# Where GpSimd's modulation units stand in a fused two-block transformer kernel

## The chip, the cores and the metric

The kernel runs on one core of one Trainium2 chip. The metric is the time of one execution in microseconds (us) on the device. Engines are called by their names: TensorE (PE, its weight loads PEld), VectorE (DVE), ScalarE (ACT), GpSimd (POOL), SyncE (SP, which here only issues transfers).

## The reference

Two transformer blocks follow each other on 256 tokens of width 1024, all in float32. Both are modulated: a vector `c` gives, through `silu(c) @ w_ada + b_ada`, the shift, the scale and the gate of every sublayer.

```python
# first block
sh1, sc1, gt1, sh2, sc2, gt2 = split(silu(c) @ w_ada + b_ada, 6)
p = project(modulate(rmsnorm(x, g_mix), sh1, sc1))       # q, k, v, g, decays, convolution, gates
x = x + gt1 * merge_branches(gla_bidir(p), conv(p))      # gated linear attention, both directions
x = x + gt2 * swiglu(modulate(rmsnorm(x, g_ffn), sh2, sc2))
x = rmsnorm(x, g_final)
# second block: nine vectors from silu(c_2) @ w_ada_2 + b_ada_2
x = x + 0.5 * g1 * swiglu(modulate(rmsnorm(x), sh1, sc1))
x = x + g2 * ((sigmoid(ga) * mla(h) + sigmoid(gb) * chunk_attention(h)) @ w_out)
x = x + 0.5 * g3 * swiglu(modulate(rmsnorm(x), sh3, sc3))
return rmsnorm(x, final_norm)
```

The change touches only how and when the products with `w_ada` and `w_ada_2` are made.

## The kernel before

Weights stream from HBM in units of 1 MB (1024 x 256 floats) through a ring of three buffers `raw`. ScalarE rounds each unit to `whi`, VectorE makes `wlo = raw - whi`, and TensorE multiplies high and low parts so that three fast products give float32 accuracy. ScalarE's split of a unit waits for the unit three before it to be used (`unit_used`), VectorE's for ScalarE's (`hi_ready`), SP's next load for VectorE's (`lo_ready`). Each engine runs a program in fixed order, and semaphores join them. The stages are: the front of the first block (decays, scans and decayed keys on ScalarE and VectorE, while TensorE makes the k and v products, lines 1398 and 2049 to 2079), the rest of the first block (45 units), its feed-forward block (11 steps of 3 units, 424 to 604 us), the first feed-forward block of the second block (to 802), its attention stage (26 units `P2`, 815 to 1004) and the last feed-forward block.

The modulation is made in 52 units of 256 columns (`ADA`), without TensorE's big products: a unit of `w_ada` lands in `ada_raw` (1 MB), is multiplied by `silu(c)`, which differs by partition and by k, and summed over k into a 1 KB piece of `acc`. TensorE later sums over the partitions with `ones` or `one`: `gate` (line 1352) for gate rows, `shift_and_scale` for columns (32 products of one column). VectorE does a unit with one product and seven multiply-adds (lines 1828 and 1832). GpSimd does it with eight instructions: four products (757), two sums (761), one (763) and one into `acc` (764).

Who does which unit before the change: GpSimd takes 0 to 15 in the first block, from the first `hlo_done` on, eight ahead of the head norms (`osq_done`) and eight behind; VectorE takes 16 to 35, one in each of the first ten steps of two feed-forward blocks; VectorE takes 36 to 39 in the attention stage at steps `ADA2_STEP`, GpSimd 40 to 47 behind them, and VectorE 48 to 51 in the last feed-forward block. All land in the one `ada_raw`, so that a load waits for the unit before it. SP issues the loads of the feed-forward blocks, GpSimd all others.

What waits for them: `gate(0)` for unit 3, `shift_and_scale(2)` for 11, `gate(1)`, at the end of the first feed-forward block, for 15, `shift_and_scale(5)`, at the end of the attention stage, for 47. In GpSimd's program the small reciprocal roots of the norms stand between the units: `split_norm(2)` behind unit 15, `split_norm(5)` behind 47, the roots of the latent norms (`lat_rs`) ahead of 36. In a feed-forward step VectorE makes two sums and the product that TensorE's next step waits for (`prod_done`), then a split, the low part of the hidden product (`low`), a split, the modulation unit and a third split.

## Time and profile before

| | us |
|---|---|
| median of 3 runs | 1218.43 |
| lowest and highest | 1217.92, 1219.31 |
| the profiled execution | 1220.7 |
| its span in the trace | 1218.9 |

| engine | busy us | share |
|---|---|---|
| TensorE, products | 1165.1 | 96% |
| TensorE, weight loads | 1040.9 | 85% |
| VectorE | 833.7 | 68% |
| ScalarE | 574.4 | 47% |
| GpSimd | 353.2 | 29% |

248.56 MB are read from HBM, 205 GB/s over the span. Line 1277 is a helper that records all products of TensorE, 1824 all of VectorE's tensor-tensor operations, 843 all of ScalarE's; stages are told apart by time. Spans on GpSimd are rough. PEclk is the clock that TensorE was granted, as a share of 2.4 GHz.

### The profile page before, as it was taken

The page shows a single profiled execution, that of the slowest core. Times are in us where ns is not written, and L with a number is a line of the kernel's source. Part 1 is how long each engine was busy: PE and PEld are TensorE (multiplying, and loading weights), DVE is VectorE, ACT ScalarE, POOL GpSimd, SP SyncE. Part 2 cuts the span into 40 slices and gives each one's busy share as a digit, 9 for nine tenths or more (in the row PEclk, how much of TensorE's full clock was granted, in tenths as well). Part 3 has the DMA queues.
Part 4 walks back from the last instruction along what each step waited for, and adds up shares of the span by engine and source line. Part 5 has one row for each costly group of instructions (what it writes and reads, how often), then busy time and mean ns, then how long its engine had stood idle before and what let it go on. Part 6 is the DMA issues. An engine that isn't in the chain of part 4 may idle for free.

```text
span 1218.9 us, 18788 instructions
## 1 busy us (share of the span) xinstructions
PE 1165.1 (96%) x7600; PEld 1040.9 (85%) x7600; DVE 833.7 (68%) x935; ACT 574.4 (47%) x734; POOL 353.2 (29%) x315
## 2 busy tenths in 40 slices
PE   6899899999999999999989999999999997999996
PEld 2599798899999988888878888889998997888885
DVE  0578555578457878878778877778655693755676
ACT  2567233354443454444464444446655543545452
POOL 1386665068577600000020000011356753000000
PEclk9889899999999999999989999989999997999998
DMA  9643545367875758877738787746754573556670
GB/s 311 217 139 120 157 146 179 117 192 226 261 247 192 242 179 275 266 242 246 260 124 287 260 261 241 254 147 219 248 178 168 191 233 112 200 180 198 216 258 35
DMA packets 192355, 250.60 MB, mean 206 GB/s; under 512 B 4763, under 2 KB 171870, under 8 KB 192158
## 3 DMA queue, kind: packets, MB, share of 16 engines
q1 hardware_dynamic: 183838, 217.44, 54.8%
q0 software_dynamic: 8448, 32.18, 7.9%
q8 instruction: 50, 0.82, 0.3%
q14 instruction: 19, 0.16, 0.0%
HBM read 248.56 MB, written 1.05 MB: 205 GB/s over the span
## 4 chain that ended last, share of the span: by engine, by line
PE 55%; POOL 17%; DVE 10%; DMA 10%; ACT 3%; issue 3%; SPq 2%; POOLq 0%; DVEq 0%; ACTq 0%
PE twin L1277 54%; DMA ada_raw<-in_w_ada 8%; POOL ada_raw L757 7%; POOL ada_raw L761 5%; DVE arena L1824 3%; DVE wlo L1824 2%; ACT arena L843 2%; POOL ada_raw L763 2%; DVE arena L1832 2%; POOL arena L764 2%; SPq L564 1%; DMA raw<-in_w_in 1%; PE twin L1345 1%; ACT whi L843 1%; DVE X L1824 1%
## 5 line engine op out<-in xcount | busy, mean ns | idle before, releaser
L1277 PE MATMUL twin<-A_both,whi 128*128 128x256 f32 (+1 forms) x2224 | 584.5, 340 | 2.5 <-DVE arena L1824 1.1
L1824 DVE TENSOR_TENSOR wlo<-raw,whi 128x2048 fp32r<-128x2048 f32 x170 | 406.5, 2393 | 166.0 <-ACT whi L843 165.8
L1277 PE MATMUL twin<-A_both,wlo 128*128 128x256 f32 x1640 | 440.0, 281 | 0.0
L843 ACT ACTIVATE whi<-raw 128x2048 fp32r<-128x2048 f32 x170 | 325.2, 1913 | 214.2 <-PE twin L1277 206.7
L1277 PEld LDWEIGHTS twin<-A_both,whi 128*128 128x128 f32 x2224 | 375.1, 191 | 45.6 <-issue 6.6
L1277 PEld LDWEIGHTS twin<-A_both,wlo 128*128 128x128 f32 x1640 | 312.3, 190 | 11.2 <-DVE A_both L1824 0.2
L757 POOL TENSOR_TENSOR ada_raw<-ada_raw,arena 128x512 f32<-128x512 f32 x96 | 137.8, 1462 | 142.1 <-DMA ada_raw<-in_w_ada 131.2
L843 ACT ACTIVATE arena<-twin 128x512 f32<-128x512 f32 (+6 forms) x168 | 89.2, 554 | 133.9 <-PE twin L1277 87.4
L843 ACT ACTIVATE arena<-arena 128x512 f32<-128x512 f32 (+7 forms) x132 | 70.0, 559 | 161.0 <-DVE arena L1824 123.7
L1277 PE MATMUL twin<-arena 128*2 128x256 f32 (+11 forms) x752 | 117.0, 319 | 19.7 <-DMA arena<-in_w_ada 11.0
L1277 PE MATMUL twin<-whi,B_hi 128*128 128x512 f32 (+2 forms) x340 | 126.6, 372 | 0.2 <-DVE B_lo L1824 0.2
L1277 PE MATMUL twin<-wlo,B_hi 128*128 128x512 f32 (+2 forms) x340 | 125.1, 368 | 0.0
L1277 PE MATMUL twin<-whi,B_lo 128*128 128x512 f32 (+2 forms) x340 | 125.1, 368 | 0.0
L1277 PEld LDWEIGHTS twin<-arena 128*128 128x128 f32 (+6 forms) x752 | 82.3, 160 | 46.3 <-issue 12.4
L1277 PE MATMUL twin<-whi,A_both 128*128 128x256 f32 x640 | 119.6, 289 | 1.5 <-DVE arena L1824 1.1
L720 POOL TENSOR_SCALAR arena<-arena 128x1 f32<-128x1 f32 x4 | 1.6, 394 | 379.9 <-ACT arena L843 379.8
L1824 DVE TENSOR_TENSOR arena<-arena,twin 128x512 f32<-128x512 f32 x92 | 62.4, 684 | 63.4 <-ACT arena L843 50.3
L1277 PEld LDWEIGHTS twin<-whi,A_both 128*128 128x128 f32 x640 | 101.7, 195 | 3.0 <-issue 2.2
L1832 DVE SCALAR_TENSOR_TENSOR arena<-ada_raw,arena 128x256 f32 (+1 forms) x196 | 95.1, 485 | 7.0
L1277 PE MATMUL twin<-wlo,A_both 128*128 128x256 f32 x320 | 91.4, 286 | 0.0
L761 POOL TENSOR_TENSOR ada_raw<-ada_raw 128x512 f32<-128x512 f32 x48 | 89.7, 1888 | 1.9
L1277 PEld LDWEIGHTS twin<-whi,B_lo 128*128 128x128 f32 x340 | 64.1, 189 | 11.2 <-issue 0.7
(128 smaller groups left out, 1170.8 us busy)
## 6 DMA issues: line engine op xcount, KB each, us to landing
raw<-in_w_in SPq DMA_DIRECT2D x49, 1024.0 KB, 5.7
raw<-in_ffn_w_in SPq DMA_DIRECT2D x44, 1024.0 KB, 5.1
ada_raw<-in_w_ada POOLq DMA_DIRECT2D x28, 1024.0 KB, 6.2
ada_raw<-in_w_ada SPq DMA_DIRECT2D x24, 1024.0 KB, 5.3
raw<-in_w_ffn_in SPq DMA_DIRECT2D x22, 1024.0 KB, 5.5
raw<-in_ffn_w_out SPq DMA_DIRECT2D x22, 1024.0 KB, 5.0
raw<-in_w_ffn_out SPq DMA_DIRECT2D x11, 1024.0 KB, 5.0
arena<-in_w_ada SPq DMA_DIRECT2D x8, 1024.0 KB, 11.7
```

The source lines that it names most:

```text
L564: sp.dma_start(ada0[j], a["w_ada"][0].rearrange("(p k) n -> p k n", k=KD)[:, :, UC * j:UC * j + UC])\
L720: link(nc.gpsimd.tensor_scalar(p[0], p[0], EPS, None, ALU.add))
L757: ins = nc.gpsimd.tensor_tensor(v[:, k:k + 2, :], v[:, k:k + 2, :], c3[:, k:k + 2, s:s + 1].to_broadcast([P, 2, UC]), ALU.mult)
L761: ins = nc.gpsimd.tensor_tensor(v[:, k:k + 2, :], v[:, k:k + 2, :], v[:, k + 4:k + 6, :], ALU.add)
L763: link(nc.gpsimd.tensor_tensor(v[:, 0:2, :], v[:, 0:2, :], v[:, 2:4, :], ALU.add))
L764: nc.gpsimd.tensor_tensor(dst, v[:, 0, :], v[:, 1, :], ALU.add).then_inc(ada_sum, 1)
L843: return nc.scalar.activation(o, i, f, **kw)
L1277: return nc.tensor.matmul(o, l, r, start=start, stop=stop, **kw)
L1345: ins = nc.tensor.transpose(bank[norm_bank(n, b)][:, c:c + P], src[:, t, P * k:P * k + P], ident)
L1824: return nc.vector.tensor_tensor(o, x, y, op)
L1832: return nc.vector.scalar_tensor_tensor(out=o, in0=x, scalar=sc, in1=y, op0=op0, op1=op1)
```

## The change

Units 12 to 15 move from the end of the first block into the first feed-forward block, where GpSimd now works at steps 0, 2, 4 and 6 beside VectorE's units 16 to 25. They land in a buffer of their own, `ada_ffn`, which is free there. In the first block GpSimd begins only when TensorE has made the transposes of the context keys (`ktc_tr`), does units 0 to 4 ahead of the head norms and 5 to 11 behind them. In the attention stage VectorE's units 36 to 39 are loaded by SP, between the weight units, and done at steps 1, 4, 6 and 8; GpSimd loads unit 40 as soon as `shift_and_scale(4)` has read `acc`, into a second buffer `ada_mix`, and from 42 on the units alternate between `ada_raw` and `ada_mix`, so that a load runs while the unit before it is worked on. No unit is added or dropped.

```diff
--- before.py
+++ after.py
@@ -118,10 +118,10 @@
 ADA_LAST = ADA_P2 + NADA2
 
 
-ADA_FFN = [n for n in range(len(ADA)) if NADA1 <= n < ADA_P2 or n >= ADA_LAST]
-ADA_MIX = [n for n in range(len(ADA)) if n not in ADA_FFN]
-ADA_DVE = [n for n in range(len(ADA)) if n in ADA_FFN or ADA_P2 <= n < ADA_P2 + 4]
+ADA_DVE = [n for n in range(len(ADA)) if NADA1 <= n < ADA_P2 + 4 or n >= ADA_LAST]
 ADA_POOL = [n for n in range(len(ADA)) if n not in ADA_DVE]
+ADA_BLOCK1 = 12
+ADA_SPARE = [n for n in ADA_POOL if ADA_P2 < n and (n <= ADA_P2 + 5 or n % 2)]
 
 LAST_STEPS = (0, NF - 4, NF - 3, NF - 2)
 
@@ -141,7 +141,7 @@
 PARTIAL = {2: 0, 5: 2}
 BROWS = 48 + 72
 
-ADA2_STEP = [1, 3, 5, 7]
+ADA2_STEP = [1, 4, 6, 8]
 
 
 def build(nc, a, out):
@@ -254,6 +254,8 @@
         XN = at3(24, TT, D)
         HF = at3(32, KD, T)
         HF1 = [at3(0, KD, T), at3(8, KD, T)]
+        ada_ffn = at3(64, KD, UC)
+        ada_mix = at3(12, KD, UC)
         sF = at(40, 512)
         hF = at(42, 512)
         yF = [at(44 + 2 * n, 512) for n in range(4)]
@@ -304,6 +306,7 @@
         pool_chain = sem("pool_chain")
         ada_landed = sem("ada_landed")
         ada_landed_p = sem("ada_landed_p")
+        ada_landed_m = sem("ada_landed_m")
         ada_mac = sem("ada_mac")
         ada_sum = sem("ada_sum")
         start_ada = [sem(f"start_ada{j}") for j in range(8)]
@@ -441,9 +444,19 @@
 
         def ada_landing(n):
 
-            if n in ADA_FFN:
-                return ada_landed, 16 * (ADA_FFN.index(n) + 1)
-            return ada_landed_p, 16 * (ADA_MIX.index(n) + 1)
+            if n in ADA_DVE:
+                return ada_landed, 16 * (ADA_DVE.index(n) + 1)
+            if n in ADA_SPARE:
+                return ada_landed_m, 16 * (ADA_SPARE.index(n) + 1)
+            return ada_landed_p, 16 * ([x for x in ADA_POOL if x not in ADA_SPARE].index(n) + 1)
+
+        def pool_rows(n):
+
+            if n < ADA_BLOCK1:
+                return ada_raw[:]
+            if n < NADA1:
+                return ada_ffn
+            return ada_mix if n in ADA_SPARE else ada_raw[:]
 
         def lin(a, i, b):
 
@@ -533,7 +546,7 @@
                         blk, c0 = ADA[n0 + m]
                         w = (a["w_ada"] if blk == 0 else a["w_ada_2"])[0].rearrange("(p k) n -> p k n", k=KD)
                         if n0 == NADA1 and m == 0:
-                            sp.wait_ge(*ada_done(n0 - 1))
+                            sp.wait_ge(*ada_done(ADA_BLOCK1 - 1))
                         else:
                             sp.wait_ge(ada_mac, lin(KD, i, KD * ada_order(n0)))
                         sp.dma_start(ada_raw[:], w[:, :, piece(UC, i, c0 - UC * m, UC)]).then_inc(ada_landed, 16)
@@ -583,8 +596,11 @@
             sp.dma_start(posi.bitcast(I32), a["positions_2"].rearrange("o (t p) -> p (o t)", p=P),
                          allow_slow_non_contiguous=True).then_inc(pos_in, 16)
             load_ffn(1)
+            load_ada(ADA_P2)
             for n2, (kind, n) in enumerate(P2):
                 load_unit(BASE_P2 + n2, kind, n)
+                if n2 - 5 in ADA2_STEP[:3]:
+                    load_ada(ADA_P2 + 1 + ADA2_STEP.index(n2 - 5))
             load_ffn(2)
             sp.wait_ge(x_ready, 6)
             sp.dma_start(finrow[1], a["final_norm_2"].partition_broadcast(P)).then_inc(fin_in, 16)
@@ -741,18 +757,15 @@
                     negative_root(rstd[:, 12 + t:13 + t], part8[:, 2 * t:2 * t + 1]).then_inc(frs_done, 1)
 
             def load_ada(n):
-                if n:
-                    pool.wait_ge(*ada_done(n - 1))
-                else:
-                    pool.wait_ge(as_mm, 1)
-                pool.dma_start(ada_raw[:], ada_source(n)).then_inc(ada_landed_p, 16)
+
+                pool.dma_start(pool_rows(n), ada_source(n)).then_inc(ada_landing(n)[0], 16)
 
             def adapt(n):
 
                 s = 0 if ADA[n][0] == 0 else 2
                 dst = acc[:, UC * ada_pos(n):UC * ada_pos(n) + UC]
                 pool.wait_ge(*ada_landing(n))
-                v = ada_raw
+                v = pool_rows(n)
                 for k in range(0, KD, 2):
                     ins = nc.gpsimd.tensor_tensor(v[:, k:k + 2, :], v[:, k:k + 2, :],
                                                   c3[:, k:k + 2, s:s + 1].to_broadcast([P, 2, UC]), ALU.mult)
@@ -792,23 +805,32 @@
             pool.dma_start(ghb, a["g_head"][0].partition_broadcast(P)).then_inc(gh_in, 16)
             for d in range(2):
                 pool.dma_start(wdec[RANK * d:RANK * d + RANK, d, :], a["w_dec_up"][0, d]).then_inc(dec_in, 16)
+            pool.wait_ge(as_mm, 1)
             load_ada(0)
-            pool.wait_ge(hlo_done, 16)
-            for n in range(8):
+            pool.wait_ge(ktc_tr, 4)
+            for n in range(5):
                 adapt(n)
+                pool.wait_ge(*ada_done(n))
                 load_ada(n + 1)
             for t in range(TT):
                 pool.wait_ge(osq_done, t + 1)
                 root(orstd[:, 4 * t:4 * t + 4], oss[:, 4 * t:4 * t + 4], HV).then_inc(orstd_done, 1)
-            for n in range(8, NADA1):
+            for n in range(5, ADA_BLOCK1):
                 adapt(n)
-                if n + 1 < NADA1:
+                if n + 1 < ADA_BLOCK1:
+                    pool.wait_ge(*ada_done(n))
                     load_ada(n + 1)
-                if n == 8:
+                if n == 5:
                     pool.wait_ge(on_done, 8)
                     gate_bias(0)
             split_norm(2)
             gate_bias(1)
+            for n in range(ADA_BLOCK1, NADA1):
+                if n > ADA_BLOCK1:
+                    pool.wait_ge(*ada_done(n - 1))
+                load_ada(n)
+                pool.wait_ge(prod_done, 2 * (n - ADA_BLOCK1) + 1)
+                adapt(n)
             twice_norm()
             gate_bias(2)
             for f in range(HR):
@@ -816,15 +838,22 @@
             ins.then_inc(inv_done, 1)
             piece_norm(1, 8, rstd_done)
             gate_bias(3)
-            load_ada(ADA_P2)
+            pool.wait_ge(as_mm, 4)
+            load_ada(ADA_P2 + 4)
             for j, w in ((0, QR), (1, KVR)):
                 pool.wait_ge(act_evac, EV2[j][1])
                 root(rs2[:, 2 * j:2 * j + 2], ss2[:, 2 * j:2 * j + 2], w).then_inc(lat_rs, 1)
-            for n in range(ADA_P2, ADA_LAST):
-                if n > ADA_P2:
-                    load_ada(n)
-                if n in ADA_POOL:
-                    adapt(n)
+            adapt(ADA_P2 + 4)
+            pool.wait_ge(*ada_done(ADA_P2 + 4))
+            load_ada(ADA_P2 + 5)
+            adapt(ADA_P2 + 5)
+            pool.wait_ge(*ada_done(ADA_P2 + 3))
+            load_ada(ADA_P2 + 6)
+            for n in range(ADA_P2 + 6, ADA_LAST):
+                if n + 1 < ADA_LAST:
+                    pool.wait_ge(*ada_done(n - 1))
+                    load_ada(n + 1)
+                adapt(n)
             split_norm(5)
             gate_bias(4)
             piece_norm(2, 14, frs_done)
```

## Rows read from the trace of the kernel before

**Rows 1.** Page, part 4: the chain that ended last, shares by line.

```profile
PE twin L1277 54%; DMA ada_raw<-in_w_ada 8%; POOL ada_raw L757 7%; POOL ada_raw L761 5%; DVE arena L1824 3%; DVE wlo L1824 2%; ACT arena L843 2%; POOL ada_raw L763 2%; DVE arena L1832 2%; POOL arena L764 2%; SPq L564 1%; DMA raw<-in_w_in 1%; PE twin L1345 1%; ACT whi L843 1%; DVE X L1824 1%
```

**Rows 2.** List of waits of the stretches 124:135 and 990:1050 us: total, times, longest.

```profile
PE twin L1398 <- DVE arena L1824: 6.1, 1, 6.1
...
PE twin L1277 <- POOL arena L764: 8.7, 1, 8.7
```

**Rows 3.** Windows: stretch, length; busy us of five engines; PEclk, DMA share, GB/s.

```profile
452.00:604.00 152.00, 151.63 (x798) 129.21 (x798) 120.35 (x138) 72.40 (x66) 0.00 (x0) 1.00 0.79 259
```

**Rows 4.** Timeline of VectorE, 116:131: start, us, engine line op, out<-in, count [idle].

```profile
116.32 0.17 DVE L2068 COPY arena<-arena 128x2 f32<-128x2 f32 x1
...
118.68 1.53 DVE L1824 TENSOR_TENSOR arena<-arena 128x510 f32<-128x510 f32 x1
120.13 1.00 DVE L2079 COPY arena<-arena 128x2 f32<-128x2 f32 x1
...
130.29 0.68 DVE L1824 TENSOR_TENSOR arena<-arena 128x512 f32<-128x512 f32 x1
```

**Rows 5.** Chain in order of time, 131:149 us: start, us, what.

```profile
131.03 3.68 PE twin L1398 x16
134.70 12.30 PE twin L1277 x96
147.00 1.75 PE twin L1398 x16
```

**Rows 6.** Timeline of TensorE at the norms n = 2 and n = 5.

```profile
415.02 3.63 PE L1277 MATMUL twin<-arena 128*128 128x1 f32 x32
419.76 3.57 PE L1345 MATMUL twin<-arena 128*128 128x128 f32 x16 [1.11 <-DVE arena L1828]
...
1012.85 6.99 PE L1277 MATMUL twin<-arena 128*128 128x1 f32 x32 [8.68 <-POOL arena L764]
1019.70 3.65 PE L1345 MATMUL twin<-arena 128*128 128x128 f32 x16
```

**Rows 7.** Timeline of GpSimd, last unit of the second block, VectorE at rest.

```profile
1003.88 4.21 POOL L757 TENSOR_TENSOR ada_raw<-ada_raw,arena 128x512 f32<-128x512 f32 x4 [7.60 <-DMA ada_raw<-in_w_ada]
1008.18 2.48 POOL L761 TENSOR_TENSOR ada_raw<-ada_raw 128x512 f32<-128x512 f32 x2
1010.74 1.26 POOL L763 TENSOR_TENSOR ada_raw<-ada_raw 128x512 f32<-128x512 f32 x1
1012.08 0.72 POOL L764 TENSOR_TENSOR arena<-ada_raw 128x256 f32<-128x256 f32 x1
```

**Rows 8.** First feed-forward block: timelines of three engines; below, a group of page part 5.

```profile
452.43 0.49 PE L1277 MATMUL twin<-A_both,whi 128*128 128x512 f32 x1 [0.37 <-DVE arena L1824]
...
515.50 0.69 DVE L1824 TENSOR_TENSOR arena<-arena 128x512 f32<-128x512 f32 x1
519.26 1.92 ACT L843 ACTIVATE whi<-raw 128x2048 fp32r<-128x2048 f32 x1 [2.20 <-PE twin L1277]
...
L1824 DVE TENSOR_TENSOR wlo<-raw,whi 128x2048 fp32r<-128x2048 f32 x170 | 406.5, 2393 | 166.0 <-ACT whi L843 165.8
```

**Rows 9.** End of the second feed-forward block: SP, VectorE, ScalarE, chain; page part 6.

```profile
782.92 17.00 SPq L504 DMA_DIRECT2D raw<-in_w_in  x4
787.83 3.61 DVE L1832 SCALAR_TENSOR_TENSOR arena<-ada_raw,arena 128x256 f32 x7
795.29 1.91 ACT L843 ACTIVATE whi<-raw 128x2048 fp32r<-128x2048 f32 x1
801.63 0.31 DVE arena L1824
...
ada_raw<-in_w_ada SPq DMA_DIRECT2D x24, 1024.0 KB, 5.3
```

**Rows 10.** Latent norms: timeline of VectorE, and the chain in order of time.

```profile
835.43 1.00 DVE L1828 TENSOR_SCALAR arena<-arena 128x256 f32<-128x256 f32 x4
...
837.75 0.45 PE twin L1708 x4
```

## The prediction

> **What bounds the kernel now.** I read the chain first: TensorE's products carry 54% of it, but GpSimd's lines 757 to 764 carry 16% and the landing of `ada_raw` 8%, so GpSimd's modulation units end some stage last [rows 1]. The list of waits says where TensorE really stood still: 8.7 us for GpSimd's last unit (L764) and 6.1 us for VectorE before the key transposes (L1398) [rows 2]. Everywhere else it is nearly gapless; in the first feed-forward block it is busy 151.63 of 152 us at full clock, and VectorE is busy 120.35 us of the same stretch while GpSimd does nothing [rows 3]. So three places decide: the front of the first block, the feed-forward block that gets new work, and the end of the second block.
>
> **Gain 1, the front.** GpSimd now multiplies through units 0 to 3 while VectorE makes the scans and decayed keys that TensorE waits for. VectorE's dense stretch from 118.68 to 130.97 us holds 8 products of 510 or 512 columns and 4 tiny copies. Undisturbed they last 0.68 and 0.17 us, so about 8 x 0.69 + 4 x 0.17 = 6.2, less the small overlaps between neighbours (some 0.07 us each), 5.5 us; they took 12.3. In that stretch one GpSimd unit of 8 instructions ran: 6.75 us of delay to VectorE per unit, 0.84 us per GpSimd instruction. Even a copy of 0.17 takes 1.00 [rows 4]. Without it that stretch alone ends near 124.2, while TensorE arrives at 124.9, and the scans before it, which other units slow in the same way, come earlier too. The stall goes whole: 6.1 us. It also left TensorE at half clock: 16 transposes took 3.68 us where the next 16 took 1.75, and 96 products took 12.30 where 0.12 each make 11.5; another 2.7 us [rows 5]. Gain 8.8 (7 to 9). Five units are now done between the transposes (then near 127 us) and the head norms (near 239): 11 us each plus 8 for each load is about 92 us, so they still fit, with 20 us over. The 7 units after that take some 21 us each as now and end near 386, 15 us before the norm.
>
> **Gain 2, into the first feed-forward block.** GpSimd's last unit there stands ahead of `split_norm(2)` and slows VectorE's sums. TensorE ends its columns at 418.65 and starts the transposes at 419.76, after a wait of 1.11 us for VectorE [rows 6]. With no unit in the way the scaled rows come before 418.6. Gain 1.2 (1 to 2.5).
>
> **Gain 3, end of the second block.** The shift and scale columns wait until 1012.85 for unit 47, and by then TensorE is at half clock: 6.99 us for 32 column products that took 3.63 at the other norm [rows 6]. With two landing buffers and an earlier start, units 42 to 47 follow each other without landing waits: an undisturbed unit is 4.21 + 2.48 + 1.26 + 0.72 = 8.7 us [rows 7], some 11.5 with VectorE in the way, so from about 879 us (after VectorE's unit 39) they end near 950. Then columns 1004.2 to 1007.8, last square near 1005.8, second rstd near 1007.1, both rows scaled by 1007.9, transposes from 1007.8 instead of 1019.7 (they are cold, 3.65 us, now; I leave them cold). Gain 11.7 (10.6, which copies the other norm's interval of 8.9 us, to 13). Gains together 21.7.
>
> **Loss 1, four units in the first feed-forward block.** They replace none of VectorE's work; they only find a place beside it. Each starts just after a product of an even step, and each step of VectorE is a dense row of splits, eight multiply-adds of the modulation and sums. In a steady step the product ends at 516.19, and TensorE, whose step begins where a down product ends and releases ScalarE's split of 519.26, asks for it at 519.2: 3 us of slack. In step 0 there is none: TensorE already waits 0.37 us at 452.43 [rows 8]. The eight GpSimd instructions fall on VectorE's row as they did in the front. Step 0 loses the whole 6.75. Unit 13 starts after step 2, where the next slack is 2.6, and costs about 6.0 - 2.6 = 3.4, since VectorE's pauses absorb part (it rests a fifth of the time [rows 3]). Units 14 and 15 cost 5.8 - 2.9 = 2.9 each. Sum 16.0. TensorE's clock fell to half after the 6.1 us stall in the front and cost 2.7 more [rows 5]; I take 2 for step 0 and nothing sure for the short ones. Loss 18. Bounds: from below, GpSimd's costs in thin stretches: all 170 splits of the kernel average 2393 ns against 2290 undisturbed [rows 8], so 17.5 us spread over 24 units, 0.7 us each; then only step 0 is hurt, loss 2 to 4 with its sums. From above, every instruction waits its full time, 8.7 a unit, loss 26. I take the value near the front's row because the row of instructions is as dense as there. The last of the four starts after step 6 and is done near 555, far ahead of the gate at 604; their loads add 4 MB to 39 (259 GB/s for 152 us) and hide, for ScalarE's splits wait on TensorE there, not on data.
>
> At this place the Trainium skill speaks against the change. After the row above (a 0.17 us copy takes 1.00 beside GpSimd): its page "SBUF — State Buffer" says in the section "SBUF: two separate sides" that VectorE and GpSimd share one port pair as an exclusive lock held for the whole instruction, and that a VectorE instruction with two SBUF inputs contends too. By full instructions the unit would cost VectorE 8.7 us instead of 6.75, and the loss would be 26 instead of 18. The trace agrees that both wait for one another; why its price is lower than whole instructions, no row shows.
>
> **Loss 2, SP's queue at the end of the second feed-forward block.** `load_ada(ADA_P2)` now stands on SP before the second block's first weights and waits for VectorE's unit 35, done at 791.44. The first weights left at 782.92 and were split by ScalarE at 795.29 [rows 9]. Now they leave near 792.1, behind 1 MB: a single landing takes 5.3 us, a second MB behind it about half of that again (an estimate), so they are there near 799.8. ScalarE's split, 4.5 us later, stands ahead of the last B_hi, VectorE's split ahead of the last B_lo, and TensorE's last down product waits for that. From 795.29 this way takes 1.9 + 2.3 + 0.7, to 800.2; the gate sums at 801.63, which TensorE releases just ahead of that product, leave 1.4 us of slack. Loss 3.1 (0 if the transfers share bandwidth well, 5 if the second weights are late too).
>
> **Loss 3, the latent norms.** Unit 40 is multiplied from 831.3 us (after the second root) where GpSimd only waited. VectorE then finishes unit 36, a split and the four scalings of 0.25 us that end at 836.4, and TensorE takes them at 837.75 [rows 10]. Five or six waits of 0.84 before them make 4.2 to 5.9, slack 1.5. Loss 4.5 (1.5 to 7). VectorE's own four units move one step later and load by SP; the splits there run two products ahead, I cost that at 0 (1 if backlog builds up). Unit 41 falls on the stretch after 852, covered by the same two products. At the merge GpSimd is now gone, which may give back half a microsecond.
>
> Sum: losses 25.6, gains 21.7, +3.9 us. The profiled execution took 1220.7 us (span 1218.9 and 1.8 around it), so 1224.6 for such a one; the median of the runs is 2.3 lower, 1218.43, so I predict **1222.4 us** (rounded up).
>
> **Rivals.**
> (a) The cover holds in the feed-forward block. Point from which it decides: VectorE's delay per unit stays under the slack of 3 us. For it: GpSimd's time in the first block's thin stretches cost splits little, as the mean of 2393 shows. Against it: the density of the step. Then loss 1 is 4, loss 3 is 1.5, loss 2 stays: 21.7 - 8.7 = 13 us faster, 1205.4.
> (b) Full waiting and cold clock. GpSimd holds VectorE off for its whole instructions, the feed-forward block loses 26: 8.7 + 6.1 + 5.8 + 5.8 [rows 7]: +11.9, 1230.3. The rule of the page named above would give this.
> (c) GpSimd is still late at the end of the second block: the change then doesn't do what it says. Waiting for VectorE's unit 39 and the loads from its own queue would have to cost 55 us more than I reckon. Gain 3 falls away: +15.6, 1234.0. The six units of 11.5 speak against it.
> (d) In between: 4.5 us of delay per unit. Loss 1 is 4.5 + 2 in step 0, then 1.9, 1.6 and 1.6, together 11.6: 2.5 us faster, 1215.9.
>
> **Numbers.** Forecast 0.42 (own range 1215 to 1229), (a) 0.30, (b) 0.15, (c) 0.05, (d) 0.08. A range of 1204 to 1233 takes in (a), (b) and (d) and leaves out (c) and tails. 0.2% (2.4 us) is what a measurement of this kernel can tell. Faster: (a), half of (d) and the lower edge of the forecast, 0.40; within: 0.17; slower: 0.43.
>
> **What would show it.** In the changed kernel: no wait at L1398, its transposes in 2 us, and GpSimd's first unit after them. VectorE's stretch of 12.3 us down to about 5.5. In the first feed-forward block TensorE's busy time per 152 us falls, with waits for VectorE's product of about 7, 3, 3 and 3 us, and VectorE's multiply-adds go from 0.5 to over 1 us in four steps. The end of the second block has no wait for L764 and its columns take 3.6 us. The first weights of the second block leave SP at about 9 us later relative to the last step. I am wrong if those four stalls are absent: then the time is that of (a). I am wrong on the other side if TensorE's clock stays low after each of them.

## The result

The changed kernel took a median of 1229.95 us (1228.82 to 1230.64), the kernel before 1218.87 us beside it: a ratio of 1.0083, 95% interval 1.0069 to 1.0097. It is slower by 0.8%. The time lies in the wide range of the forecast (1204 to 1233) and at the edge of its own (1215 to 1229), but the size of the change was wrong: 4 us of loss were forecast and 10 measured by the ratio (0.0083 of 1218.9), 11 by the medians. The two profiled spans are 7.9 us apart (1226.8 against 1218.9); the profiled execution after the change was the fastest of its four.

Line numbers move by 13 or 29 in the changed kernel: 1277 is 1306, 1398 is 1427, 1824 is 1853, 1828 is 1857, 1832 is 1861, 757 is 770, 764 is 777, 1612 (transposes of the attention jobs) is 1641, 1708 (latents) is 1737, 1729 (rotations of q and k) is 1758. The experiments shift them by a few more or fewer; what a row is stays plain from its operands. First the list of TensorE's waits of the changed kernel (total, times, longest).

```profile
PE twin L1306 <- DVE arena L1853: 12.5, 7, 6.6
...
PE twin L1306 <- DVE B_lo L1853: 5.7, 5, 3.3
PE twin L1737 <- DVE arena L1857: 5.5, 1, 5.5
...
PE twin L1641 <- ACT arena L872: 3.0, 1, 3.0
PE twin L1758 <- DVE arena L1853: 2.6, 1, 2.6
```

The waits for L764 and at the key transposes [rows 2] are gone; five others, all for VectorE or for ScalarE behind it, have come. **Where they stand** shows best if the span is cut where the transposes of each norm end (from TensorE's timeline, the last such row's start plus its length). The last stretch behind norm 5 is 195.4 to 196.4 us in all kernels of this document.

| kernel | norm 2 ends | first feed-forward | second feed-forward | attention stage |
|---|---|---|---|---|
| before | 423.3 | 197.7 | 194.1 | 208.2 |
| after | 410.8 | 213.6 | 198.1 | 208.3 |

So the first block won 12.5 us, the feed-forward blocks lost 15.9 and 4.0, and the attention stage, which was to win 11.7, came out level (0.1 more): something took 11.8 us there.

**The front.** Chain in order of time, and VectorE's timeline, of the changed kernel:

```profile
123.19 1.75 PE twin L1427 x16
124.93 11.52 PE twin L1306 x96
136.45 1.75 PE twin L1427 x16
```

```profile
107.83 0.68 DVE L1853 TENSOR_TENSOR arena<-arena 128x510 f32<-128x510 f32 x1
108.43 0.16 DVE L2108 COPY arena<-arena 128x2 f32<-128x2 f32 x1
...
112.32 0.69 DVE L1853 TENSOR_TENSOR arena<-arena 128x512 f32<-128x512 f32 x1
```

VectorE's stretch of 12.3 us [rows 4] lasts 5.2, from 107.83 to 113.01, and TensorE stops nowhere; the second transposes end at 138.20 in place of 148.75 [rows 5].

**The first feed-forward block.** Timelines of GpSimd's unit 12, of VectorE's unit beside it and of TensorE's next step; then the windows 446:454, 519:527 and 440:606 (as rows 3):

```profile
425.11 8.58 POOL L770 TENSOR_TENSOR arena<-arena 128x512 f32<-128x512 f32 x4 [16.36 <-DVE arena L1853]
433.77 2.72 POOL L774 TENSOR_TENSOR arena<-arena 128x512 f32<-128x512 f32 x2
436.57 1.35 POOL L776 TENSOR_TENSOR arena<-arena 128x512 f32<-128x512 f32 x1
438.00 0.80 POOL L777 TENSOR_TENSOR arena<-arena 128x256 f32<-128x256 f32 x1
```

```profile
433.88 6.76 DVE L1861 SCALAR_TENSOR_TENSOR arena<-ada_raw,arena 128x256 f32<-128x256 f32 x7
```

```profile
446.18 0.79 PE L1306 MATMUL twin<-A_both,whi 128*128 128x512 f32 x1 [6.56 <-DVE arena L1853]
```

```profile
446.00:454.00 8.00, 7.82 (x30) 6.75 (x31) 7.44 (x10) 2.71 (x3) 0.00 (x0) 0.62 1.07 350
519.00:527.00 8.00, 7.59 (x35) 6.58 (x36) 7.47 (x9) 3.12 (x4) 0.00 (x0) 0.79 1.07 350
440.00:606.00 166.00, 155.16 (x793) 131.86 (x794) 141.87 (x143) 73.10 (x68) 42.30 (x27) 0.96 0.79 262
```

Both engines stretch: GpSimd's unit works 13.5 us (8.7 with VectorE at rest [rows 7]), VectorE's seven multiply-adds 6.76 instead of 3.61 [rows 9]. TensorE waits 6.56 us, and the clock granted behind that is 0.62, down from full. Three more waits follow, at 483.58 (1.17), 519.41 (2.31) and 555.67 (1.18). Behind the one of 2.31 us the clock falls too (0.79). Against the same products of the kernel before, TensorE loses 8.9 us around the first wait, 1.4 around the second, 4.1 around the third and 1.4 around the fourth, together 15.8 of the 15.9.

**The second block.** First weights of the attention stage on SP; the latents on three engines; the columns of norm 5:

```profile
795.71 0.57 SPq L521 DMA_DIRECT2D ada_raw<-in_w_ada  x1
796.32 12.43 SPq L517 DMA_DIRECT2D raw<-in_w_in  x4
```

```profile
837.07 8.23 DVE L1861 SCALAR_TENSOR_TENSOR arena<-ada_raw,arena 128x256 f32<-128x256 f32 x7
...
848.49 1.46 DVE L1857 TENSOR_SCALAR arena<-arena 128x256 f32<-128x256 f32 x4
...
861.58 7.38 DVE L1861 SCALAR_TENSOR_TENSOR arena<-ada_raw,arena 128x256 f32<-128x256 f32 x7
868.88 3.55 DVE L1853 TENSOR_TENSOR arena<-arena 128x256 f32<-128x256 f32 x12
```

```profile
849.61 1.11 PE L1737 MATMUL twin<-arena 128*128 128x128 f32 x4 [5.46 <-DVE arena L1857]
...
871.15 0.65 PE L1758 MATMUL twin<-arena 128*96 128x128 f32 x4 [2.62 <-DVE arena L1853]
```

```profile
1024.52 3.63 PE L1306 MATMUL twin<-arena 128*128 128x1 f32 x32
```

GpSimd's unit 40 (837.57 to 849.1) more than doubles VectorE's unit 36, ahead of the four scalings of the latents; unit 41 (856.3 to 867.6) doubles VectorE's unit 37, ahead of the twelve operations of the rotation. The columns take 3.63 us with no wait, as forecast.

### The profile page after: what moved, and what is told of

It reads as the page before. It is cut to its first block, busy times and chain, and to the rows that moved or that the text cites. A ratio compares the mean times of both kernels' runs of the same rounds, so it can differ in the third digit from the quotient of the medians.

```text
span 1226.8 us, 18792 instructions
## 1 busy us (share of the span) xinstructions
PE 1168.0 (95%) x7600; PEld 1042.0 (85%) x7600; DVE 843.6 (69%) x935; ACT 573.8 (47%) x734; POOL 347.2 (28%) x311
## 4 chain that ended last, share of the span: by engine, by line
PE 75%; DVE 13%; ACT 3%; issue 3%; DMA 3%; SPq 2%; POOL 0%; DVEq 0%; POOLq 0%; ACTq 0%
PE twin L1306 72%; DVE arena L1861 5%; DVE wlo L1853 4%; DMA raw<-in_w_in 2%; ACT whi L872 2%; DVE arena L1853 2%; SPq L577 1%; ACT arena L872 1%; DMA raw<-in_w_ffn_in 1%; PE twin L1374 1%; DVE arena L1857 1%; DVE B_lo L1853 1%; PE twin L1641 0%; DVE X L1853 0%; DVE X L1861 0%
## 5 line engine op out<-in xcount | busy, mean ns | idle before, releaser
L1306 PE MATMUL twin<-A_both,whi 128*128 128x256 f32 (+1 forms) x2224 | 592.6, 343 | 13.4 <-DVE arena L1853 12.0
L1306 PEld LDWEIGHTS twin<-A_both,whi 128*128 128x128 f32 x2224 | 380.5, 194 | 58.4 <-issue 18.6
L1306 PEld LDWEIGHTS twin<-A_both,wlo 128*128 128x128 f32 x1640 | 316.0, 193 | 11.0
L770 POOL TENSOR_TENSOR ada_raw<-ada_raw,arena 128x512 f32<-128x512 f32 x60 | 80.6, 1372 | 144.4 <-PE twin L1427 76.2
L1861 DVE SCALAR_TENSOR_TENSOR arena<-ada_raw,arena 128x256 f32 (+1 forms) x196 | 116.1, 593 | 7.0
L1306 PEld LDWEIGHTS twin<-arena 128*128 128x128 f32 (+6 forms) x752 | 79.6, 155 | 39.0 <-issue 13.6
L770 POOL TENSOR_TENSOR arena<-arena 128x512 f32<-128x512 f32 x36 | 59.3, 1675 | 86.4 <-DVE arena L1853 80.5
L1306 PEld LDWEIGHTS twin<-whi,B_hi 128*128 128x128 f32 x340 | 64.4, 189 | 13.9 <-DVE wlo L1853 4.1
```

Of the source, the lines that this page charges most:

```text
L770: ins = nc.gpsimd.tensor_tensor(v[:, k:k + 2, :], v[:, k:k + 2, :], c3[:, k:k + 2, s:s + 1].to_broadcast([P, 2, UC]), ALU.mult)
L1306: return nc.tensor.matmul(o, l, r, start=start, stop=stop, **kw)
L1861: return nc.vector.scalar_tensor_tensor(out=o, in0=x, scalar=sc, in1=y, op0=op0, op1=op1)
```

## The experiments

All start from the changed kernel but the last two. Ratios are to the kernel before, in the same sessions; the changed kernel stands at 1.0083.

### Only the loads of units 12 to 15

```diff
-                adapt(n)
+                pool.wait_ge(*ada_landing(n))
+                nc.gpsimd.tensor_tensor(acc[:, UC * n:UC * n + UC], ada_ffn[:, 0, :], ada_ffn[:, 1, :],
+                                        ALU.add).then_inc(ada_sum, 1)
             twice_norm()
```

> The changed kernel; of GpSimd's units 12 to 15 in the first feed-forward block only the load and the last of eight instructions are left (so gate 1 is wrong). Theory (VectorE is held off while GpSimd works, TensorE then waits for its product): the waits of 6.6, 1.2, 2.3 and 1.2 us for VectorE's product and the half clock behind the first go away, the block is left about as early as before, 15 to 17 us are won: 1213 to 1215 us. Rival (the 4 MB of extra loads slow the ring of weights): the loads are still there, 0 to 3 us are won, 1227 to 1230. The wait of 4.37 us of ScalarE for a weight unit would stay in either case if the loads cause it.

Measured: 1215.46 us, ratio 0.9952 (0.9927 to 0.9976). The block takes 197.8 us, as before the change, and the loads of 4 MB are still there. The loss is made by GpSimd's work, not by its data. (This kernel leaves out seven of the eight instructions of these units, so its gate 1 lacks most of the sum.)

### The same instructions on half the columns

```diff
-                v = pool_rows(n)
+                w = UC // 2 if ADA_BLOCK1 <= n < NADA1 else UC
+                v = pool_rows(n)[:, :, 0:w]
```

The last of the eight instructions keeps its whole width.

> The changed kernel; seven of the eight GpSimd instructions of each of units 12 to 15 work on half of the columns (gate 1 is wrong), their count and their starts stay. Theory A (the delay of VectorE goes with the time that GpSimd works): each unit holds VectorE 3.4 to 4 us instead of 6.75 to 7, the first stall is 3.5, the others 0 to 0.5, no half clock: 9 to 12 us won, 1218 to 1221. Theory B (a price per instruction, as the 0.84 us an instruction of my prediction was counted): the waits stay as they are, 0 to 2 us won, 1228 to 1230.

Measured: 1218.39 us, ratio 0.9986 (0.9961 to 1.0011); the block takes 200.7 us. Timelines of TensorE and VectorE, and the window 443:451:

```profile
443.38 0.49 PE L1308 MATMUL twin<-A_both,whi 128*128 128x512 f32 x1 [3.23 <-DVE arena L1855]
```

```profile
432.72 5.12 DVE L1863 SCALAR_TENSOR_TENSOR arena<-ada_raw,arena 128x256 f32<-128x256 f32 x7
```

```profile
443.00:451.00 8.00, 7.62 (x44) 6.69 (x45) 7.48 (x9) 3.69 (x4) 0.00 (x0) 1.00 1.06 344
```

One wait of 3.23 us is left of four, with full clock in the window behind it (the last row, before the two shares of transfers). Theory A holds: the delay goes with the time that GpSimd works, not with its instructions. From product to product, step 0 is 17.7 us here and 21.0 in the changed kernel (424.33 to 445.35), where the units' own undisturbed time is about 4.7 (half of seven instructions and the last whole) and 8.7 us.

### Odd steps

```diff
-                pool.wait_ge(prod_done, 2 * (n - ADA_BLOCK1) + 1)
+                pool.wait_ge(prod_done, 2 * (n - ADA_BLOCK1) + 2)
```

> The changed kernel; units 12 to 15 start one step later (steps 1, 3, 5, 7 in place of 0, 2, 4, 6). Theory (step 0 costs most because TensorE has no slack there, 0.37 us of wait in the kernel before, later steps have about 3 us): the first stall falls from 6.6 to about 3.4 us and its half clock goes, 3 to 6 us won, 1224 to 1227. Rival (each unit costs the same wherever it stands): within 1 us of the changed kernel, 1229 to 1231.

Measured: 1227.91 us, ratio 1.0069 (1.0043 to 1.0095), not told apart from the changed kernel; the block takes 211.9 us, 1.7 less. The first wait did fall:

```profile
462.57 0.79 PE L1306 MATMUL twin<-A_both,whi 128*128 128x512 f32 x1 [4.10 <-DVE arena L1853]
```

The next three are 1.18, 2.31 and 1.18 us, the same as before, and the mean clock of 440:606 is 0.97 against 0.96. So step 0's missing slack was worth 2.5 us of wait, but the half clock came all the same. Both theories miss: the median lies between their ranges.

### The front's start undone

```diff
-            pool.wait_ge(ktc_tr, 4)
+            pool.wait_ge(hlo_done, 16)
             for n in range(5):
```

> The changed kernel; GpSimd begins its first unit at the first hlo_done, as in the kernel before, not at the key transposes. Theory (these units slow VectorE's scans and decayed keys): the wait at the key transposes of 6.1 us comes back with the half clock, the time rises by the 8.8 to 10.5 us of the front, to 1239 to 1240.5. Rival (the gain came from elsewhere in the front, as the order of the first load, or is given back before the head norms): a rise under 3 us.

Measured: 1240.24 us, ratio 1.0156 (1.0089 to 1.0222). The wait of 6.1 us at the key transposes is back, norm 2 ends at 421.9 in place of 410.8. The gain of the front hangs on this one start.

### SP's order in the second block

```diff
-            load_ada(ADA_P2)
             for n2, (kind, n) in enumerate(P2):
                 load_unit(BASE_P2 + n2, kind, n)
+                if n2 == 1:
+                    load_ada(ADA_P2)
```

> The changed kernel; on SP the load of unit 36 stands behind the first two weight units of the second block's attention stage in place of ahead of them. Theory (SP waits for VectorE's unit 35 with those weights queued behind it): the first weights leave about 9 us earlier, TensorE's wait of 3.3 us for B_lo goes, 3 us won (2 to 3.5), 1226.5 to 1228. Rival (the wait at the block's end is VectorE's or ScalarE's own and hidden otherwise, or the later load of unit 36 makes its step late): within 1 us, 1229 to 1231.

Measured: 1226.47 us, ratio 1.0061 (1.0047 to 1.0074). SP issues the first two weights at 786.62, the second feed-forward block takes 194.9 us instead of 198.1, and the wait of 3.3 us for B_lo is gone. The theory holds.

### Units 40 and 41 held back

```diff
+            pool.wait_ge(lat_lo, 1)
             adapt(ADA_P2 + 4)
...
+            pool.wait_ge(rope_done, 2)
             adapt(ADA_P2 + 5)
```

> The changed kernel; GpSimd's unit 40 waits until VectorE has made the low part of the latents (lat_lo), unit 41 until both rotations are made (rope_done 2). Theory (these two units hold VectorE off ahead of the latent norms and of the transposes of q and k): the waits of 5.5 and 2.6 us for VectorE go, 4.2 + 4.8 = 9 us of the 12 lost in the attention stage come back, 1220 to 1222. Rival (VectorE's own unit 37, now a step later and right ahead of the rotation, is the cause of the second): 4.2 us come back, 1225 to 1226.5. Rival 2 (neither): 1229 to 1231.

Measured: 1226.59 us, ratio 1.0061 (1.0045 to 1.0076); the attention stage takes 205.5 us, 2.8 less. TensorE's timeline:

```profile
863.15 0.64 PE L1760 MATMUL twin<-arena 128*96 128x128 f32 x4 [2.16 <-DVE arena L1855]
...
881.14 0.51 PE L1308 MATMUL twin<-whi,A_both 128*128 128x256 f32 x2 [3.52 <-DVE wlo L1855]
```

By the rotation 8.0 us are won (863.15 against 871.15), near the 9 of the theory, but not where it said. The wait of 5.46 us at the latents is gone, and with it the half clock behind it (1.00 in the window 846:854 here, 0.63 in 849:857 of the changed kernel). The rotation's own wait is only 0.5 us shorter (2.16 against 2.62), for unit 40, held back, now works from 847.9 to 859.1 beside VectorE's unit 37. Then unit 41, from 865 to 878, lies on VectorE's unit 38 and two splits, and a wait of 3.52 us for a low part stands where none was; the wait for ScalarE behind it is 3.7 instead of 3.0. At the latents the cause was right; held back, the two units do their harm later.

### VectorE's steps as before

```diff
-ADA2_STEP = [1, 4, 6, 8]
+ADA2_STEP = [1, 3, 5, 7]
```

> The changed kernel; VectorE's units 36 to 39 stand at steps 1, 3, 5, 7 of the attention stage as before the change, in place of 1, 4, 6, 8. Theory (GpSimd's units are the cause of the loss there): within 2 us of the changed kernel, 1228 to 1231. Rival (unit 37 at step 4, ahead of the rotation, is what makes the transposes of q and k late): 4 to 5 us won, 1225 to 1226.

Measured: 1232.55 us, ratio 1.0102 (1.0086 to 1.0119); the attention stage takes 211.5 us, 3.2 more. By the time the rival falls, and the theory holds nearly. The trace grants the rival a part: with unit 37 at step 3 the wait at the rotation is 0.22 us instead of 2.62. But the rotation's twelve operations, now beside GpSimd's unit 41, take 7.39 us instead of 3.55, and a wait of 2.16 us for a low part and more waits for ScalarE follow. So unit 37 at step 4 costs only together with a unit of GpSimd, and moving it away moves the cost.

### All sixteen in the first block, two buffers

```diff
-ADA_BLOCK1 = 12
+ADA_BLOCK1 = 16
...
+            load_ada(6)
             for n in range(5, ADA_BLOCK1):
+                if n > 5 and n + 1 < ADA_BLOCK1:
+                    pool.wait_ge(*ada_done(n - 1))
+                    load_ada(n + 1)
                 adapt(n)
-                if n + 1 < ADA_BLOCK1:
-                    pool.wait_ge(*ada_done(n))
-                    load_ada(n + 1)
```

Even units from 6 on land in `ada_ffn`.

> The changed kernel; units 12 to 15 are back in the first block, where units 5 to 15 now alternate between two landing buffers (ada_raw and ada_ffn), and none is in the first feed-forward block. Theory (11 units of 12 to 13 us without landing waits fit between the head norms at 239 us and the norm at 408; TensorE is the bound there and VectorE has slack): the 16 us of the feed-forward block come back whole, 1213 to 1215. Rival (denser GpSimd work holds VectorE off so that TensorE waits in the first block): part of it is given back there, 1217 to 1228.

Measured: 1231.67 us, ratio 1.0101 (1.0085 to 1.0116). The feed-forward block is back at 197.6 us, but norm 2 ends at 427.6, 16.8 later. A window of the changed kernel's trace and the same of this one's; then VectorE's and TensorE's rows of this one:

```profile
260.00:280.00 20.00, 19.48 (x162) 19.31 (x162) 17.49 (x15) 9.69 (x10) 12.42 (x9) 1.00 0.73 235
```

```profile
260.00:280.00 20.00, 14.99 (x124) 14.82 (x123) 19.90 (x12) 9.03 (x10) 19.29 (x13) 0.93 0.78 263
```

```profile
240.69 6.57 DVE L1856 TENSOR_TENSOR wlo<-raw,whi 128x2048 fp32r<-128x2048 f32 x1 [2.87 <-ACT whi L875]
```

```profile
279.41 0.77 PE L1309 MATMUL twin<-whi,A_both 128*128 128x256 f32 x2 [5.00 <-DVE arena L1856]
```

GpSimd is busy 19.29 of 20 us instead of 12.42, VectorE 19.90, TensorE 14.99 instead of 19.48. From 300 to 380 us, where VectorE has fewer instructions, GpSimd was as dense (19.0 to 19.4 of 20) and TensorE lost 0.6 us in all. At 400.26 comes a second wait of 4.98 us, beside the last units. The kernel before also had its last units at the end of this block, but in one buffer; a window of its trace and the same of this kernel's, where TensorE stands within 1.4 us at the same products:

```profile
380.00:400.00 20.00, 20.00 (x158) 19.04 (x158) 14.54 (x14) 9.23 (x7) 14.41 (x9) 1.00 0.61 205
```

```profile
380.00:400.00 20.00, 15.28 (x116) 13.99 (x114) 15.65 (x12) 6.25 (x6) 19.61 (x12) 1.00 0.43 139
```

With one buffer GpSimd works 14.41 of 20 us there and TensorE never stops; with two, 19.61 and 15.28. So the landing waits that the second buffer took away had been VectorE's pauses for catching up. That is read from these windows; no run puts a pause back beside a second buffer.

### Three edits of the second block

```diff
-            adapt(ADA_P2 + 4)
-            pool.wait_ge(*ada_done(ADA_P2 + 4))
-            load_ada(ADA_P2 + 5)
-            adapt(ADA_P2 + 5)
-            pool.wait_ge(*ada_done(ADA_P2 + 3))
-            load_ada(ADA_P2 + 6)
-            for n in range(ADA_P2 + 6, ADA_LAST):
+            for n in range(ADA_P2 + 4, ADA_LAST):
```

with SP's order and VectorE's steps of the two kernels above; even units land in `ada_mix`.

> The changed kernel with three edits in the second block: SP loads unit 36 behind the first two weight units, VectorE's units 36 to 39 stand at steps 1, 3, 5, 7, and GpSimd begins units 40 and 41 only when VectorE's unit 39 is done (the two landing buffers stay). Theory (the loss of the attention stage is GpSimd's two units falling on VectorE's dense stretch from 831 to 885 us, wherever in it): no wait of VectorE's latents, rotations or splits is seen by TensorE before 890 us, 3 us of the queue and 9 to 10 of the 12 us of the stage come back, GpSimd ends near 986, ahead of the norm: 1216 to 1219. Rival (VectorE's units one step later or the fourth MB of loads are the cause): 3 us from the queue and at most 3 more, 1223 to 1227. Rival 2 (GpSimd, with 16 us less, is late at the norm): a wait for L777 and 1220 or more.

Measured: 1226.01 us (1216.95 to 1230.23), ratio 1.0034 (1.0015 to 1.0053). Three of the twelve runs lie at 1217 to 1219, nine at 1224 to 1230, and the trace is that of the slowest; what parts them is open. Its waits in the attention jobs, and a window:

```profile
PE twin L1636 <- ACT arena L867: 10.4, 4, 4.3
```

```profile
880.00:900.00 20.00, 17.10 (x139) 16.48 (x137) 12.65 (x12) 9.98 (x23) 18.89 (x16) 1.00 0.63 199
```

Nothing waits before 880 us any more, but the stage takes 211.2 us. The eight units without a pause now lie on the attention jobs, where TensorE, ScalarE and VectorE hand small tiles to one another; TensorE waits 10.4 us for ScalarE, which had its input late from VectorE. The kernel before has the same eight units behind VectorE's unit 39, in one buffer, and waits 1.7 us there for ScalarE. VectorE is busy only 12.65 of 20 us in the window. Its busy share alone does not tell where GpSimd is free; my theory, and the three quarters in the next expectation, had it so.

### The same, and no unit in the feed-forward block

Units 0 to 5 ahead of the head norms, 6 to 8 in one buffer, 9 to 15 in two:

```diff
-ADA_BLOCK1 = 12
+ADA_BLOCK1 = 16
+ADA_FFNB = [9, 11, 13, 15]
```

> As the kernel with three edits in the second block, and no unit in the first feed-forward block: units 0 to 5 stand ahead of the head norms, 6 to 8 behind them in one landing buffer as before, 9 to 15 alternate between two. Theory (GpSimd costs TensorE time only where VectorE is busy more than some three quarters: 240 to 300 us, not 300 to 385, where VectorE is busy half of the time): the 16 us of the feed-forward block come back at a cost of 0 to 3 in the first block, 1199 to 1205, faster than both kernels. Rival (two buffers make GpSimd dense and that alone costs TensorE, as 18 us were lost when units 5 to 15 all did so): 1209 to 1219.

Measured: 1222.85 us, ratio 1.0019 (1.0010 to 1.0027). The theory fails the way the rival says, and by more than its 1209 to 1219. The first feed-forward block takes 198.0 us, but norm 2 ends at 423.8: TensorE was busy 60 of 60 us from 300 to 360 with GpSimd at 19.1 to 19.4 of each 20, and 32.6 of 40 from there to 400, where each product's result goes through VectorE into the next one's input.

### Units cut up and spread over the steps

From the kernel before:

```diff
-            pool.wait_ge(hlo_done, 16)
-            for n in range(8):
+            pool.wait_ge(ktc_tr, 4)
+            for n in range(6):
...
+            for n in range(ADA_BLOCK1, NADA1):
+                load_ada(n)
+                s0 = 1 + 3 * (n - ADA_BLOCK1)
+                adapt(n, [s0] * 3 + [s0 + 1] * 3 + [s0 + 2] * 2)
             twice_norm()
             gate_bias(2)
+            pool.wait_ge(as_mm, 3)
+            for n in (40, 41):
+                pool.dma_start(ada_ffn, ada_source(n)).then_inc(ada_landed_m, 16)
+                adapt(n, [NF + 1 + 4 * (n - 40) + x // 2 for x in range(8)])
```

`adapt` waits ahead of each of its eight instructions for the product of the step that the list gives; `ADA_BLOCK1` is 13.

> The kernel before with GpSimd's units placed by what the runs so far showed. First block: units 0 to 5 ahead of the head norms, from the key transposes on, 6 to 12 behind them, all in one landing buffer with its pauses. Units 13 to 15 in the first and 40 and 41 in the second feed-forward block, in a buffer of their own and cut up: at most three (first block) or two (second) of a unit's eight instructions behind one step's product. Attention stage as in the kernel before, but GpSimd has only 42 to 47 there. Theory (GpSimd costs TensorE nothing as long as the delay it gives VectorE in a stretch stays below TensorE's lead there; three instructions are about 2.5 us against 2.6 to 3 us a step): no wait of TensorE over 1 us in the feed-forward blocks, the front's 10.5, the norm's 1.7 and the 11.7 at the end of the second block are all won: 1194 to 1201, faster than both kernels. Rival (the delays add up over the steps, or each instruction costs TensorE its own time wherever it stands): 40 instructions by 0.84 less nothing, up to 30 us, given back: 1205 to 1225.

Measured: 1200.78 us (1198.71 to 1202.17), ratio 0.9837 (0.9822 to 0.9853): faster than both kernels by 1.6% and 2.4%. GpSimd's timeline of two steps; TensorE's longest wait in the steps of the first feed-forward block but the last; the window 652:800:

```profile
440.70 5.53 POOL L771 TENSOR_TENSOR arena<-arena 128x512 f32<-128x512 f32 x3 [31.21 <-DVE arena L1850]
457.76 1.04 POOL L771 TENSOR_TENSOR arena<-arena 128x512 f32<-128x512 f32 x1 [11.54 <-DVE arena L1850]
458.89 4.92 POOL L776 TENSOR_TENSOR arena<-arena 128x512 f32<-128x512 f32 x2
```

```profile
526.38 0.49 PE L1303 MATMUL twin<-A_both,whi 128*128 128x512 f32 x1 [0.72 <-DVE arena L1850]
```

```profile
652.00:800.00 148.00, 148.00 (x774) 125.83 (x772) 128.87 (x136) 68.00 (x63) 30.84 (x31) 1.00 0.78 255
```

In the second feed-forward block two instructions a step cost TensorE nothing (194.2 us, 194.1 before the change). In the first, with up to three, it takes 202.5 us, 4.8 more than before, with waits up to 0.9 us and full clock. The attention stage, with six units of GpSimd in one buffer ended at 966.8, takes 196.2 us, 12.0 less than before.

### The same five units at once

From the spread kernel:

```diff
-                adapt(n, [s0] * 3 + [s0 + 1] * 3 + [s0 + 2] * 2)
+                adapt(n, [s0] * 8)
...
-                adapt(n, [NF + 1 + 4 * (n - 40) + x // 2 for x in range(8)])
+                adapt(n, [NF + 1 + 4 * (n - 40)] * 8)
```

> The kernel with the units spread over the feed-forward steps, but each of the five units runs its eight instructions at once behind one step's product (steps 1, 4, 7 of the first feed-forward block, 1 and 5 of the second), at the same count, buffers and loads. Theory (what counts is the delay of VectorE inside one step against TensorE's lead there): five waits of 2 to 4 us for VectorE's product come back, as the 14 us of four units started at odd steps, 12 to 17 us slower than the spread kernel: 1213 to 1218. Rival (the spread kernel is fast for having fewer units in the blocks, not for cutting them up): within 3 us of it, 1199 to 1204.

Measured: 1217.02 us, ratio 0.9983 (0.9971 to 0.9996), 16 to 18 us slower than the spread kernel.

```profile
463.12 0.79 PE L1303 MATMUL twin<-A_both,whi 128*128 128x512 f32 x1 [4.18 <-DVE arena L1850]
```

One wait for each of the five units is there, 4.18, 1.56, 1.92, 4.20 and 1.56 us, together 13.4, in the two blocks, which take 209.3 and 202.6 us: 6.8 and 8.4 more than with the units cut up. Count, buffers, loads and order are the same. What differs is how much of GpSimd's work falls within one step.

The stages of all that bear on it, cut as above:

| kernel | norm 2 ends | first feed-forward | second feed-forward | attention stage |
|---|---|---|---|---|
| only loads in the block | 410.5 | 197.8 | 198.1 | 209.0 |
| half the columns | 411.2 | 200.7 | 197.9 | 208.8 |
| odd steps | 412.1 | 211.9 | 198.1 | 209.0 |
| SP's order | 410.4 | 213.5 | 194.9 | 209.2 |
| 40 and 41 held back | 411.1 | 213.5 | 198.1 | 205.5 |
| steps as before | 411.0 | 213.8 | 198.3 | 211.5 |
| all in the first block | 427.6 | 197.6 | 198.3 | 209.2 |
| three edits | 413.5 | 213.3 | 194.5 | 211.2 |
| no unit in the block | 423.8 | 198.0 | 194.4 | 209.7 |
| spread | 411.2 | 202.5 | 194.2 | 196.2 |
| at once | 412.3 | 209.3 | 202.6 | 194.6 |

## Why the prediction was right, and where it was not

**Gain 1** (8.8): 10.5 at the second transposes. The mechanism is shown by undoing it, and the size was about right. VectorE ends the stretch at 113.0, not near 124.2, since the scans ahead of it had been slowed in the same way, but that wins nothing more: TensorE comes only at 123.19. Some 1.5 us of the 10.5 arise between 71 and 77 us, where TensorE waits for nobody: from 70 to 76 us its granted clock is 0.72 in the kernel before and 1.00 in the changed one. The odd-steps and the spread kernel have the same front and 0.72 there, and win 9.3 and 9.2 us from 60 us on. So this part belongs to the one execution and not to the change.

**Gain 2** (1.2): norm 2 ends 12.5 us earlier, 2.0 more than the front gives. Of these, 0.5 come at 285 us, where a wait of 1.07 us for VectorE shrinks to 0.52, and 1.5 at the norm, within its bounds.

**Gain 3** (11.7): the wait for GpSimd and the half clock at norm 5 are gone, and the stage of the spread kernel is 12.0 us shorter than before. The size was right. Rival (c) is out: GpSimd's last unit ended at 969.15, far ahead of the norm.

**Loss 1** (18): 15.9. Step 0 was to cost 6.75 + 2 = 8.75 us and cost 8.9: a wait of 6.56 us, and the rest half clock (0.62 in the 8 us behind it, worth up to 3.0). The delay per unit, 6.25 us in step 0 (the lead of 12.5 us over the kernel before falls to 6.25 from one product to the next), is near the 6.75 taken from the front. The three later units were to cost 3.4, 2.9 and 2.9 us of waits and no clock, together 9.2; they cost 1.4, 4.1 and 1.4, together 6.9. Their waits were 1.17, 2.31 and 1.18, shorter than forecast, but behind the second of them the clock fell (0.79 in 8 us, worth 1.7), which the sum had at nothing. Two errors cancelled in part here. The price of 0.84 per instruction is not a law, as half-width instructions cost half. Rival (a) is out, and so is the 26 of rival (b), though its total of 1230.3 happens to be near the result.

**Loss 2** (3.1): 4.0 by the stage, 3.2 by undoing it alone. The mechanism is shown and the size about right; the other 0.8 of the stage stays unexplained.

**Loss 3** (4.5): this step failed. The attention stage would take 208.2 - 11.7 = 196.5 us without any loss (the spread kernel shows 196.2); it took 208.3, so 11.8 were lost. The latents are late by 4.5 us more than what was carried in (849.61 against 837.75 is a lag of 11.9, norm 4 ended 7.4 behind), as forecast. But the half clock behind that stall (0.63 in 849:857, worth 2 to 3 us) had no term, and "unit 41 falls on the stretch after 852, covered by the same two products" was wrong: at the rotation the lag is 16.7, 4.8 more, made of that half clock and of a wait of 2.62 us, since unit 41 and VectorE's unit 37 ran side by side ahead of its twelve operations. And units 42 to 47, counted as 11.5 us each and at no cost to TensorE, were given no term at all: GpSimd at 18.9 to 19.4 of each 20 us from 900 to 960 made VectorE and ScalarE late in the attention jobs (3.0 us at L1641, where the kernel before waits 1.7). About 2.5 of the 11.8 are left for this and for the clock behind the rotation's wait. The three-edit kernel, with all eight units there, shows 10.4 us of such waits. The prediction looked at which waits the second buffer removes and not at what those waits had been good for.

The sum with the measured terms: 12.5 + 11.7 - 15.9 - 4.0 - 11.8 = -7.5, and 0.5 in the last stretch makes, up to rounding, the 7.9 of the spans. The other 2 to 3 us of the ratio and of the medians are in no trace. That the time fell in the range says little: the range was 29 us wide, the forecast gave faster and slower nearly the same chance (0.40 and 0.43), and the loss of the attention stage was missed by 7 us.

In the front the row showed less delay than GpSimd's whole time, and the unit in step 0 cost VectorE 6.25 us for 8.7 us of undisturbed work, while it stretched itself by 4.8. The Trainium skill, page "SBUF — State Buffer", section "SBUF: two separate sides", has the shared ports as a lock held for a whole instruction. That both engines wait for one another is what the trace shows. The loss of 26 that I worked out from that rule did not come. That alone does not refute the rule, since VectorE rests a fifth of the time there [rows 3].

## What to carry to other kernels

Work given to GpSimd beside a busy VectorE is not free even where TensorE is the bound: ask how much delay one step can take before TensorE asks for VectorE's result, and cut GpSimd's work so that no step gets more. Eight instructions at once cost 3.5 to 4.2 us a unit, two a step nothing, here a difference of 1.5% of the kernel. A landing wait of an engine off the critical path can be the pause in which another catches up; before removing it with a second buffer, look at who shares its time.

## What the hardware showed unexpectedly

One split of VectorE (128 x 2048), 2.29 us alone, took 2.87 us beside GpSimd in one place and 6.57 us in another. In the long case (240.69 to 247.26, in the kernel with all sixteen units in the first block) four products of GpSimd lay wholly inside it, at 1.01 us each, no longer than with VectorE at rest [rows 7]:

```profile
241.07 4.04 POOL L772 TENSOR_TENSOR ada_raw<-ada_raw,arena 128x512 f32<-128x512 f32 x4
245.19 4.49 POOL L776 TENSOR_TENSOR ada_raw<-ada_raw 128x512 f32<-128x512 f32 x2
```

The rows fit a split that stands until the fourth product is done and then works for its 2.29 us (245.11 + 2.29 = 247.40, near its end), while GpSimd's two sums behind the products take 4.49 us, 2.0 more than the 2.48 at rest. The same shape stands at 376.59: a split of 5.93 us beside four products of 4.04 us that end at 380.36. That is inferred from the times alone. In the feed-forward step four such products took 8.58 us and the splits beside them 2.87 and 3.12. So who waits for whom differs from place to place; what decides it was not found, and spans on GpSimd are rough.

The clock granted to TensorE falls from the upper to the lower of its levels for part of the window behind a stall of 4 to 7 us (mean 0.62 in the 8 us behind the 6.56, 0.64 behind the 4.18 of the kernel with the units at once). For shorter stalls their length does not tell: the 2.31 us at 519.41 left 0.79, one of 2.28 us in the kernel with the front undone left 1.00 (530:538), and one of 3.23 us left 1.00. What decides there is open. Two of the four units of the changed kernel cost more than their waits in this way.
